# Attention weights in units of 256 columns, the first input turned before it is normed, and a convolution moved to VectorE

## What is computed

```python
hn = rmsnorm(h, norm_mix[i])                     # x * rsqrt(mean(x^2) + eps) * g
qkv = hn @ w_qkv                                 # 1024 x 3072, layers 0 and 1
...
a = jax.nn.softmax(s, axis=-1); a = a[0] - lam * a[1]      # layer 0
...
q, k, v, f_logit, b_gate, c_gate, u = jnp.split(xn @ w_in, split_at, axis=-1)   # layer 2
y_attn = forgetting_attention(q, k, v, log_f)
y_conv = b_gate * causal_depthwise_conv(c_gate * u, conv_w)
y = concat([head_rms_norm(y_attn), head_rms_norm(y_conv)])
h = h + y @ w_out
```

## Time and profile before

| | |
|---|---|
| median of 3 runs | 1067.57 us |
| the profiled execution | 1067.28 us, its span from first to last instruction 1065.5 us |
| TensorE busy | 1006.3 us, 94% |
| VectorE, ScalarE, GpSimd busy | 643.7, 494.1, 141.4 us |
| chain that ended last | TensorE 82%, VectorE 8%, ScalarE 5%, issue 3%, DMA 2% |
| mean granted TensorE clock | 0.988 |

### The profile page before, as it was taken

One profiled execution on the slowest core, in us unless ns is written; L12 is line 12 of the kernel. 1 busy time (PEld: TensorE's weight loads), 2 busy tenths in 40 slices (PEclk: granted clock), 3 DMA queues, 4 the chain that ended last, 5 costly groups with the idle time before them and its releaser, 6 DMA issues.

```text
span 1065.5 us, 13456 instructions
## 1 busy us (share of the span) xinstructions
PE 1006.3 (94%) x5354; PEld 848.1 (80%) x5354; DVE 643.7 (60%) x967; ACT 494.1 (46%) x708; POOL 141.4 (13%) x219
## 2 busy tenths in 40 slices
PE   1998799999999999999999999999999999999996
PEld 1987578888888898877888888888789878888885
DVE  4766867655655876544765655568644677555553
ACT  3545545444444654545454444455644345444431
POOL 5000099550000000000000000012502400000000
PEclk9999999999999999989999999999999999999998
DMA  9663246965555556322385566545632336555511
GB/s 270 208 231 98 67 117 170 279 205 181 181 191 198 175 197 202 119 80 80 99 275 170 188 196 196 178 142 179 205 119 83 116 119 232 185 176 197 181 57 40
DMA packets 102414, 175.27 MB, mean 165 GB/s; under 512 B 5905, under 2 KB 53009, under 8 KB 102353
## 3 DMA queue, kind: packets, MB, share of 16 engines
q1 hardware_dynamic: 95936, 165.69, 48.0%
q0 software_dynamic: 6208, 8.08, 3.1%
q10 hardware_dynamic: 208, 0.66, 0.2%
HBM read 173.35 MB, written 1.05 MB: 164 GB/s over the span
## 4 chain that ended last, share of the span: by engine, by line
PE 82%; DVE 8%; ACT 5%; issue 3%; DMA 2%; SPq 0%; DVEq 0%; ACTq 0%
PE bank L871 25%; PE bank L873 25%; PE bank L872 24%; DVE wl L1290 2%; DMA raw<-in_da_w_qkv_dram 2%; PE bank L1041 2%; ACT wh L572 2%; PE bank L886 1%; ACT prob L629 1%; PE bank L1018 1%; DVE prob L1406 1%; PE bank L993 1%; ACT pt L646 1%; PE bank L967 1%; PE bank L996 1%
## 5 line engine op out<-in xcount | busy, mean ns | idle before, releaser
L1290 DVE TENSOR_TENSOR wl<-raw,wh 128x2048 fp32r<-128x2048 f32 x156 | 359.8, 2314 | 225.9 <-ACT wh L572 225.6
L572 ACT ACTIVATE wh<-raw 128x2048 fp32r<-128x2048 f32 x156 | 295.7, 1910 | 122.8 <-PE bank L873 113.7
L871 PE MATMUL bank<-wh,xh 128*128 128x512 f32 (+1 forms) x728 | 290.6, 399 | 6.0 <-issue 3.5
L873 PE MATMUL bank<-wh,xl 128*128 128x512 f32 (+1 forms) x728 | 284.8, 391 | 0.0
L872 PE MATMUL bank<-wl,xh 128*128 128x512 f32 (+1 forms) x728 | 284.6, 391 | 0.0
L871 PEld LDWEIGHTS bank<-wh,xh 128*128 128x128 f32 (+1 forms) x728 | 136.7, 188 | 34.6 <-issue 6.2
L873 PEld LDWEIGHTS bank<-wh,xl 128*128 128x128 f32 (+1 forms) x728 | 136.4, 187 | 30.2
L872 PEld LDWEIGHTS bank<-wl,xh 128*128 128x128 f32 (+1 forms) x728 | 136.9, 188 | 27.6
L871 PE MATMUL bank<-xh,wh 128*128 128x256 f32 (+1 forms) x416 | 122.9, 295 | 10.3 <-DVE xl L1369 10.2
L871 PE MATMUL bank<-wh,ah 128*128 128x512 f32 x320 | 127.4, 398 | 0.0
L873 PE MATMUL bank<-wh,al 128*128 128x512 f32 x320 | 125.1, 391 | 0.0
(11 more groups left out here) (219 smaller groups left out, 877.2 us busy)
## 6 DMA issues: line engine op xcount, KB each, us to landing
raw<-in_w_ff_dram SPq DMA_DIRECT2D x32, 1024.0 KB, 5.1
raw<-in_ffn_w_gate_dram SPq DMA_DIRECT2D x44, 512.0 KB, 4.0
raw<-in_ffn_w_up_dram SPq DMA_DIRECT2D x44, 512.0 KB, 5.0
raw<-in_ffn_w_down_dram SPq DMA_DIRECT2D x22, 1024.0 KB, 4.9
raw<-in_da_w_qkv_dram SPq DMA_DIRECT2D x12, 1024.0 KB, 7.3
raw<-in_na_w_qkv_dram SPq DMA_DIRECT2D x12, 1024.0 KB, 5.2
raw<-in_w_in_dram SPq DMA_DIRECT2D x12, 1024.0 KB, 5.2
raw<-in_ple_w_gate_dram SPq DMA_DIRECT2D x8, 1024.0 KB, 5.1
```

The lines of the kernel that those rows point to most:

```text
L572: nc.scalar.activation(wh[:, i % RING, :], raw[:, i % RAW, :], ACT.Copy).then_inc(s_hi, 1)
L871: nc.tensor.matmul(dst, lh, rh, start=start, stop=False, skip_group_check=True)
L873: return nc.tensor.matmul(dst, ll, rh, start=False, stop=stop, skip_group_check=True)
L1290: nc.vector.tensor_tensor(wl[:, i % RING, :], raw[:, i % RAW, :], wh[:, i % RING, :].bitcast(F32), ALU.subtract).then_inc(s_lo, 1)
```

## The change

1. Layers 0 and 1: but for the first 512 columns of q, the weights of q, k, v come in units of 256 columns and all 1024 rows, in the order q0 (2 units), k0, v0, k1, v1, q2, k2, v2, q3, k3, v3 (`PARTS`). A unit of v is now 48 matmuls of 256 columns. Each unit's result is one PSUM bank of a ring of four. There are 18 slots of half a unit from v0 on; steps 0 to 7 stand behind slots 1 to 8, 8 to 11 behind 10 to 13, 12 and 13 behind 16 and 17; steps 14 to 18 follow.
2. In a slot VectorE and ScalarE do the step first and then the split.
3. Layer 0 works on x times gain, without the root: TensorE turns raw x (L917), ScalarE and VectorE scale by the gain's column as they write `xh` and `xl`. The 1/rms comes in where q and k leave PSUM (VectorE) and v (ScalarE), as layer 1 had it. The first two units are split in quarters. The broadcast of the first gain falls away; the loads of constants wait for the second unit.
4. Layer 2: the wait for q, k and the running sum moves from the second unit of v to the first score, which moves behind slot 1. VectorE squares the 1/rms once in place of GpSimd's second multiplication of c, and convolves in place of GpSimd.

```diff
+        PARTS = [("q", 0), ("k", 0), ("v", 0), ("k", 1), ("v", 1), ("q", 2), ("k", 2), ("v", 2), ("q", 3), ("k", 3), ("v", 3)]
...
+        STEPS = [[]] + [[s] for s in range(8)] + [[], [8], [9], [10], [11], [], [], [12], [13]]
+        TAIL = 14
...
-        STEPS_2 = [[0], [1], [2]] + [[2 * n - 3, 2 * n - 2] for n in range(3, 11)] + [[]] * 4
+        STEPS_2 = [[], [0], [1, 2]] + [[2 * n - 3, 2 * n - 2] for n in range(3, 11)] + [[]] * 4
...
+                if i == 0:
+                    for k in range(4):
+                        sp.dma_start(dst[:, k, :], units[0][0][2][:, k, :]).then_inc(s_first[k], 16)
+                    continue
...
-            load_gain(1)
+            pool.dma_start(meta_s, t["meta_tokens_2"]).then_inc(s_meta, 16)
+            pool.dma_start(meta_gain, t["norm_mix_g_2"][0].partition_broadcast(META)).then_inc(s_meta, 16)
...
+            pool.wait_ge(s_raw[1], landed[1])
...
-            for m in range(4):
-                pool.wait_ge(s_c, m + 1)
-                nc.gpsimd.tensor_tensor(c_s[:, m, :], c_s[:, m, :], r_cols[:, :], ALU.mult).then_inc(s_cscaled, 1)
...
+            act.dma_start(gain_rows[:, :], t["norm_mix"][0].rearrange("(k p) -> k p", p=P)).then_inc(s_gain_first, 16)
+            act.wait_ge(s_gturned, 1)
+            nc.scalar.activation(gain_cols[:, :], bank[3][:, 0:KD], ACT.Copy).then_inc(s_gcols, 1)
...
+                for slot, steps in enumerate(STEPS):
+                    part, c = part_of_slot(slot)
+                    for s in steps:
+                        attention_step(l, s)
+                    split_to(first[part, l, c] + 4)
...
+            def first_pair(cols):
+                for kh in range(2):
+                    w_hi, w_lo = (w[:, kh, :].rearrange("p (k n) -> p k n", k=4) for w in (wh, wl))
+                    for b in range(TB):
+                        need("mix0", b, kh)
+                    for k in range(4):
+                        pe.wait_ge(s_lo, 4 * kh + k + 1)
+                        for m in range(4):
+                            ins = three(pair(0)(m), (w_hi[:, k, m * P:(m + 1) * P], w_lo[:, k, m * P:(m + 1) * P]),
+                                        x_of(4 * kh + k, cols), kh == 0 and k == 0 and m % 2 == 0, kh == 1 and k == 3)
+                    ins.then_inc(s_used, 1)
...
+                        if s == 0:
+                            wait(pe, q_scaled, 2, 1)
+                            wait(pe, k_ready, 2, 1)
+                            pe.wait_ge(s_kcum, 2)
...
+            def convolve(m):
+                dve.wait_ge(s_cu, m + 1)
+                link(nc.vector.tensor_scalar(y_s[:, m, :], cu[:, m, META:META + S], conv_w[:, 2, m:m + 1], None, ALU.mult))
+                for w in (1, 0):
+                    ins = nc.vector.scalar_tensor_tensor(out=y_s[:, m, :], in0=cu[:, m, META - 2 + w:META - 2 + w + S],
+                                                         scalar=conv_w[:, w, m:m + 1], in1=y_s[:, m, :],
+                                                         op0=ALU.mult, op1=ALU.add)
+                    link(ins)
```

More of the change, by code:

```diff
@@ L742, in _ @@
-                for s in range(SLOTS - 1, 19):
+                for slot, steps in enumerate(STEPS):
[3 more added lines that the diff above has]
+                    split_to(first[part, l, c] + 4)
+                    if slot % 2 == 1 and part == "q":
+                        q_out(c)
+                    if slot % 2 == 1 and part == "v" and l == 0:
+                        v_copy(c)
+                turns_hi(f"att{l}", 0)
@@ L743, in _ @@
+                for s in range(TAIL, 19):
                     attention_step(l, s)
@@ L881, in turn @@
             def turn(name, b, c):
[L883 removed]
+                if c == 1 and name != "mix0" and not name.startswith("att"):
                     need(name, b, 0)
@@ L1118, in _, with quarter @@
-                run(qkv_units(0))
+                    pe.wait_ge(s_gain_first, 16)
+                    nc.tensor.transpose(bank[3][:, 0:KD], gain_rows[:, :], ident[0:KD, 0:KD]).then_inc(s_gturned, 1)
+                    for c in range(2):
+                        for b in range(TB):
+                            pe.wait_ge(s_x[b], 16)
+                            turn(mix, b, c)
+                x_cols = slice(X0, XP)
+                def quarter(part, c):
+                    u = first[part, l, c]
+                    dst = part_bank(part, c)
+                    at = PARTS.index((part, c))
+                    if at >= 3:
+                        before, bc = PARTS[max(at - 4, 0)]
+                        wait(pe, {"q": q_ready, "k": k_ready, "v": v_ready}[before], l, bc)
+                    w_hi, w_lo = (w.rearrange("p (k n) -> p k n", k=KD) for w in unit(u))
+                    for i in range(2):
+                        half = slice(S * i, S * i + S)
+                        for k in range(KD):
+                            if part == "v":
+                                need(mix, i, k // 4)
+                                ins = three(dst[:, half], x_of(k, tok(i)), (w_hi[:, k, :], w_lo[:, k, :]),
+                                            i == 0 and k == 0, k == KD - 1)
+                            else:
+                                ins = three(dst[:, half], (w_hi[:, k, i * P:(i + 1) * P], w_lo[:, k, i * P:(i + 1) * P]),
+                                            x_of(k, x_cols), i == 0 and k == 0, k == KD - 1)
+                        if i == 1:
+                            ins.then_inc(s_used, 1)
+                        yield
```

373 lines of the change are left out of this document (192 added, 181 removed).

## The result

The changed kernel takes 1051.53 us (median of 4 runs, 1049.74 to 1052.78) against 1067.62 us for the kernel before on the same chip (4 runs, 1065.63 to 1067.71). The ratio is 0.9849, with a 95% interval of 0.9829 to 0.9870. The sign was right. The size was not: 16.1 us were won where 30.9 were forecast, and 1051.5 lies above the upper end of the range, 1045. The profiled execution took 1049.74 us with a span of 1047.8, so by the two traces the gain is 17.7 us. It was the fastest of the four, and the others show a lower mean clock (0.986 to 0.988 against 0.989). A "slow stretch" is here a stretch in which TensorE's granted clock is 0.50, which is 1.2 GHz and not 2.4. One of 3.4 us costs 1.7, and one or two more or less are most of the spread.

The account below looks back on a forecast made before the run. TensorE, busy 1006.3 of 1065.5 us, bounds the kernel, so only its idle time, slow time and own work count. Terms -21.6 (head and layer 0), -4.5, -4.7, -0.1 sum to -30.9: 1036.7 us, range 1029 to 1045.

Parts of the forecast that it names:

- The first matmul: Head: with x and the first units loaded first, the first matmul of weights starts at 10.0 us, against 24.56 before.
- v's cost: Layers 0 and 1: v's 192 matmuls of 256 columns replace 96 of 512, +1.1 us in each layer, weight loads hidden.
- the rival with weight loads end to end: v in layers 0 and 1: matmuls of 256 columns don't overlap, +35.5 us in place of +2.2, time 1070.0; 3%.
- Layer 2's start: Layer 2: v's second unit starts at once, without the 3.53 us idle and low clock behind it; -4.7 us (-6 to -1).
- the saving of VectorE's small operations and the loss of it to the convolution: Layer 2: heads come 3.5 us earlier, then convolution delays the turn's low part by 2.4; sum -0.1 us (-2 to +3).
- By the queue: Head: VectorE's queue finishes roots and meta rows at some 25 us, TensorE needs them at 23.5; wait 1.2 us (0 to 4).
- the 2.0 us of half rate: Head: the first matmuls run at half rate, as before, adding 2.0 us (0 to 4).
- Waits and unit borders: Layer 0 up to step 14's score: 3.0 us (1 to 6); the split order behind step 8's 1.79 us wait goes.
- After step 14 I change nothing: Layer 0 behind step 14's score: order of work unchanged, so the 21.6 us gained by then is kept.
- I give back 1.0: Layer 1: of 5.5 us gained up to step 14, 1.0 is lost to a shorter slow stretch; -4.5 us (-7 to 0).
- VectorE's queue late in layer 0: Layer 0: k0, v0 and the first steps could each wait 1 to 2 us for VectorE; +5 us, time 1041.5; 14%.
- the signs that I had named: Wrong if first matmul after 14 us, scores wait for VectorE in most slots, or low clock exceeds 3.4 us in a layer.

## Why the prediction was right and wrong

**Right.** The first matmul (10.0 forecast, 9.93 measured), the first two units behind it, and v's cost: its matmuls start 0.12 apart, so the rival with weight loads end to end is out. Layer 2's start (-4.7 forecast; -5.2), the saving of VectorE's small operations and the loss of it to the convolution (-0.1; about +0.4) were right in mechanism and in sum.

**Wrong, step one: "By the queue: ... some 25. TensorE needs them at 23.5: a wait of 1.2".** The meta product ends at 25.65, as worked out. But q0's matmuls end at 21.7, since the 2.0 us of half rate that I kept at the start did not come; the wait was 4.03, and some 3 us were lost in the slow stretch behind it, which the sum put at nothing. Less those 2.0, that makes score 0 3.3 us later than the sum's 38.2 (41.51; small terms make up the rest). The experiments show that naming this wait did not find the bound: taken away, it comes back at k0, then at the row maxima, and costs the same or more.

**Wrong, step two: "Waits and unit borders: 3.0 (1 to 6) ... That order goes".** From score 0 to 14 the sum has 66.9 us and the trace 73.39. The term itself came out at some 7.9 us, which is what is left of 73.39 after 16 slots of 2.88, the steps and the turn, and 5.2 of it stand at the scores of the steps 12 (3.7) and 13 (1.5, in a slow stretch). The old order of splits and steps was read as the cause of the wait in the earlier trace rows, and its going as a gain. It is a loss: the kernel that undoes it is 5.7 us faster, and saves 4.5 us from score 3 to 14. I followed VectorE's queue and not ScalarE's, whose split now stood behind an exponential that waits for VectorE. Beside it, a step costs 1.44 us in place of 1.33, which is 1.4 over the stretch.

**Wrong, step three: "After step 14 I change nothing" and "I give back 1.0".** Layer 1 was 4.0 us faster up to step 14, where 5.5 were forecast: from step 8 on a step costs some 2.1 us, not 1.95, and step 8 waited 0.74 us for k2. It gave 1.9 back, not 1.0, in the steps 14 and 15, which wait 0.93 us for row maxima and 0.99 more than before for a copy. Layer 0 gave back 1.0 in the same place. That these steps came straight behind the turn was in the code.

**The rivals.** VectorE's queue late in layer 0 (14%, +5 us) is nearest to what happened, at twice its price (9.8 us) and mostly in another place. It named the head: there the meta rows cost 3.3 us, while k0, v0 and the first steps did not wait. The other 6.5 are lost later, at the end of layer 0's attention above all. It was sized from single waits of 1 to 2 us, and not from the low clock that stands behind a long one, nor from both queues together. Of the signs that I had named, the low clock did come back for more than 3.4 us in layer 0 (6.8 us in the head alone). Scores that wait in most slots did not come: up to step 14 three waited, at the steps 8, 12 and 14.

**What is left open.** 5 us or more of layer 0: with the splits ahead score 14 comes at 110.7 to 115.7, against the forecast's 105.1. Whether a mixed order, or the order of one engine alone, wins part of it was not run.

## What to carry to other kernels

When two engines in strict order each hold one half of a job (here a split) and one half of a loop (here row maxima and exponentials), write out both queues side by side before judging an order: work whose inputs are ready goes ahead of work that waits for the other engine. Then look at each stretch by itself, since here the same order saved 4.5 us late in layer 0 and cost 1.4 us or more in its first steps. When a wait is shortened, take the next two things that the same engine owes into the sum, since in this head three edits in a row only moved the wait. And price a stop like the ones here (3.3 to 4.1 us) with the slow stretch that the windows showed behind it, 1.7 to some 3 us more.

The fastest versions measured here are not told apart (1042.0 to 1043.2 us). The simplest of them keeps the change's load order and units, undoes its order of steps and splits, and moves half of the convolution behind the turn: 1042.0 us.

## What the hardware showed beside that

- TensorE's first weight matmuls ran at the full rate here, where those of the kernel before started 0.21 us apart, at half rate, up to 29.0. Here x's turns run from 4.4 to 8.3 us and 1.62 us of idle time precede the first matmul; before, 9.83 us did. The granted clock reads 1.00 in both stretches, so the half rate at a program's start shows in the distance of the starts alone.
- Slow stretches come and go with the same code: layer 1's tail (474 to 480) has one in the traces of some edits of the head and of layer 2 and none in the changed kernel's. A stop of 2.6 us ahead of step 2's score was followed by 6.8 us at 1.2 GHz in one trace (1045.18 us) and by none in another.
- GpSimd took 1.69 us for one product of 128x384 with a constant (8 in 13.54), where VectorE took 0.28 (8 in 2.24) in the changed kernel. From the timeline of the kernel with the table on GpSimd:

```profile
7.54 13.54 POOL L472 TENSOR_SCALAR kb_reg<-kb_reg 128x384 f32<-128x384 f32 x8
```
